# Stage borders of a two-layer streaming encoder: where the last block's norm sums go, how early the scaling runs, and how many residual slots there are

## What is computed

```python
for i in range(DEPTH):
    h = rms_norm(x, norm_g[i, 0])
    o = mixer(h)                                   # GLA for i = 0, SWA for i = 1
    x = x + rms_norm(o, norm_g[i, 1])
    h = rms_norm(x, norm_g[i, 2])
    x = x + rms_norm(squared_relu_mlp(h, w_up, w_down), norm_g[i, 3])
```

## Time and profile before

| | us |
|---|---|
| median of 3 runs | 2623.77 (2623.68 to 2635.75) |
| the profiled execution, whole | 2626.12 |
| its span | 2624.3 |
| TensorE busy in the span | 2509.7 (96%) |
| VectorE, ScalarE, GpSimd busy | 910.4, 842.0, 554.4 |
| mean granted TensorE clock | 0.98 |

### The profile page before, as it was taken

The page is one execution under the profiler, slowest core; times in us unless marked ns, Lnnn a source line. Parts: engine busy times, 40 slices in busy tenths (PEclk is TensorE's granted clock), DMA queues, the critical chain, the costliest instruction groups (busy, mean ns, idle before and its releaser), DMA issues.

```text
span 2624.3 us, 41637 instructions
## 1 busy us (share of the span) xinstructions
PE 2509.7 (96%) x17454; PEld 2370.0 (90%) x17454; DVE 910.4 (35%) x1785; ACT 842.0 (32%) x1666; POOL 554.4 (21%) x314
## 2 busy tenths in 40 slices
PE   6999999998999999999998999899899999999997
PEld 5878877798999999999998877689899999999996
DVE  6455454426322222222226344415422222212225
ACT  4445444526221221121125455536411211211121
POOL 1101010115221211221214211114312211212213
PEclk9999999999999999999998999899999999999998
DMA  3101010114111111111114200013211111111113
GB/s 107 41 10 47 26 40 17 43 45 147 62 46 42 47 40 48 40 48 40 60 33 135 67 26 26 29 33 116 82 47 43 41 47 41 47 40 48 40 61 125
DMA packets 63088, 139.05 MB, mean 53 GB/s; under 512 B 8688, under 2 KB 39920, under 8 KB 62960
## 3 DMA queue, kind: packets, MB, share of 16 engines
q1 hardware_dynamic: 33984, 103.60, 12.1%
q10 hardware_dynamic: 28976, 33.64, 4.2%
HBM read 117.81 MB, written 19.40 MB: 52 GB/s over the span
## 4 chain that ended last, share of the span: by engine, by line
PE 78%; ACT 3%; DVE 3%; issue 2%; ACTq 1%; DMA 0%; POOL 0%; DVEq 0%; POOLq 0%
PE banks L217 52%; PE banks L197 18%; PE banks L1860 1%; PE banks L1380 1%; PE banks L1361 1%; ACTq L339 1%; ACT norm_sq L464 1%; PE banks L1348 1%; PE banks L1388 0%; DVE norm_acc_x L542 0%; PE banks L2011 0%; PE banks L369 0%; PE banks L2014 0%; PE banks L1995 0%; ACT w_hi L153 0%
## 5 line engine op out<-in xcount | busy, mean ns | idle before, releaser
L160 POOL TENSOR_TENSOR w_lo<-w_raw,w_hi 128x1024 fp32r<-128x1024 f32 x168 | 414.9, 2473 | 1870.1 <-ACT w_hi L153 1870.1
L197 PE MATMUL banks<-h_hi,w_hi 128*128 128x384 f32 (+1 forms) x1224 | 432.8, 354 | 6.3 <-ACT gla_v_tok L2110 3.0
L197 PE MATMUL banks<-h_lo,w_hi 128*128 128x384 f32 (+1 forms) x1224 | 409.9, 335 | 0.0
L197 PE MATMUL banks<-h_hi,w_lo 128*128 128x384 f32 (+1 forms) x1224 | 409.1, 334 | 0.0
L153 ACT CAST w_hi<-w_raw 128x1024 fp32r<-128x1024 f32 x180 | 186.9, 1046 | 461.6 <-DMA w_raw<-in_units 461.6
L217 PE MATMUL banks<-h_hi,w_hi 128*128 128x384 f32 (+1 forms) x1368 | 301.8, 329 | 0.0
L217 PE MATMUL banks<-h_hi,w_lo 128*128 128x384 f32 (+1 forms) x1368 | 301.4, 328 | 0.0
L217 PE MATMUL banks<-h_lo,w_hi 128*128 128x384 f32 (+1 forms) x1368 | 301.4, 328 | 0.0
L217 PE MATMUL banks<-mlp_a_hi,w_hi 128*128 128x384 f32 (+1 forms) x1344 | 296.5, 329 | 1.5 <-issue 1.3
L217 PE MATMUL banks<-mlp_a_lo,w_hi 128*128 128x384 f32 (+1 forms) x1344 | 295.1, 327 | 0.0
L217 PE MATMUL banks<-mlp_a_hi,w_lo 128*128 128x384 f32 (+1 forms) x1344 | 295.0, 327 | 0.0
(11 more groups left out here) (199 smaller groups left out, 3183.4 us busy)
## 6 DMA issues: line engine op xcount, KB each, us to landing
w_raw<-in_units SPq DMA_DIRECT2D x180, 512.0 KB, 3.5
x_scratch<-y ACTq DMA_DIRECT2D x48, 192.0 KB, 1.9
norm_x<-x_scratch ACTq DMA_DIRECT2D x48, 192.0 KB, 2.7
x_scratch<-y ACTq DMA_DIRECT2D x24, 160.0 KB, 1.8
norm_x<-x_scratch ACTq DMA_DIRECT2D x24, 160.0 KB, 2.6
y<-in_x SPq DMA_DIRECT2D x16, 192.0 KB, 4.9
norm_x<-in_x ACTq DMA_DIRECT2D x16, 192.0 KB, 2.7
out_y<-y SPq DMA_DIRECT2D x16, 192.0 KB, 3.2
```

Source lines behind the costliest of these rows:

```text
L160: c.nc.gpsimd.tensor_tensor(c.w_lo[:, s], c.w_raw[:, s], c.w_hi[:, s].bitcast(F32), ALU.subtract).then_inc(self.ready, 1)
L197: mm = chip.nc.tensor.matmul(out, w, x, start=(first and n == 0), stop=(last and n == 2))
```

## The change

1. In borders 1 to 4, block 2's sums and its spread move from bank 5 to the squares' bank 4 (`norm_bank`), and the wait of `bank_left` goes.
2. On TensorE, in the middle borders: block 1's spread one place later; the second norm's sums of block 0 at the end of the last wave and not behind the first job of the next stage; behind that job the spread of it and block 2's sums; block 2's spread behind job (0, 1) and not (0, 3); block 1's second sums behind (0, 3) and not (1, 0).
3. On DVE and ACT the scaling and splitting of block 1 starts earlier in the last wave, `root_x(0)` and `inverse_x(0)` stand ahead of the last two weight units or one of them, `root(2)` and `inverse(2)` stand in job (0, 0), and block 2's steps begin in job (0, 1). For b > 0 the DVE sums the squares of x and makes the low part one step later behind the scaling (`lag`).
4. In borders 1 and 3 the odd tiles of block 0 are also split by DVE and not POOL (`low_by_vector`).
5. In border 4 there are nine slots for x: five more in the MLP's buffer `act`, loaded by `load_more_x` before the last wave. Block 1's steps begin after job (2, 3) and not (2, 4), and `root(2)` stands ahead of the remaining `high` calls.

```diff
-    X_SLOTS = 4
+    X_SLOTS, X_MORE = 4, 5
+    def norm_bank(self, b):
+        return SQ_BANK if b == 2 and not self.first else RS_BANK + b % 2
     def low_by_vector(self, b, k):
-        return self.first or (b > 0 and k % 2 == 1)
+        return self.first or (k % 2 == 1 and (b > 0 or not self.after_mlp))
     def sums(self, pe, b):
-        if b == 2:
-            self.bank_left(pe)
+        if b == 2 and self.first:
+            pe.wait_ge(self.s.scaled, KT)
...
-        if (b, q) == (2, 3):
+        if (b, q) == ((2, 3) if self.last else (2, 4)):
             self.spread(pe, 1)
+        if self.middle and (b, q) == (2, 7):
+            self.sums_x(pe, 0)
     def tensor_in_first_wave(self, pe, b, j):
         if (b, j) == (0, 0):
-            self.sums_x(pe, 0)
-        if (b, j) == (0, 1):
             self.spread_x(pe, 0)
-        if (b, j) == (0, 2):
             self.sums(pe, 2)
-        if (b, j) == (0, 3):
+        if (b, j) == (0, 1):
             self.spread(pe, 2)
...
     def scalar_before_first_wave(self, act, next_unit):
         ws.high(act, next_unit + 2)
-        self.high(act, 1, 0)
+        self.root_x(act, 0)
+        if self.after_mlp:
+            self.high(act, 1, 2)
         ws.high(act, next_unit + 3)
-        self.high(act, 1, 1)
-        self.root_x(act, 0)
-        self.high(act, 1, 2)
         self.high(act, 1, 3)
+        self.high(act, 1, 4)
         self.keep_block(act, 0)
...
     def scalar_after_all(self, act):
-        for k in range(6, KT):
+        self.root(act, 2)
+        for k in range(4, KT - 1):
             self.high(act, 1, k)
-        self.root(act, 2)
-        for k in range(KT - self.X_SLOTS):
-            self.high(act, 2, k)
```

More of the change, by code:

```diff
@@ L294, in gained @@
     def gained(self, b, k):
-        n = self.added * (NB * KT - KT) + self.count_alike(b, k)
+        n = sum(self.LOWS_BY_GPSIMD[:self.norm]) + self.count_alike(b, k)
         return n, self.s.sq[:, n % 2, 0:WIDTH[b]]
@@ L304, in h_ready @@
         if self.low_by_vector(b, k):
-            engine.wait_ge(self.s.lo_done_v, n if self.first else NB * KT + self.added * KT + n)
+            engine.wait_ge(self.s.lo_done_v, sum(self.LOWS_BY_VECTOR[:self.norm]) + n)
         else:
-            engine.wait_ge(self.s.lo_done, self.added * (NB * KT - KT) + n)
+            engine.wait_ge(self.s.lo_done, sum(self.LOWS_BY_GPSIMD[:self.norm]) + n)
     def bank_free(self, pe, j):
@@ L674, in vector_in_last_wave @@
                 self.steps(dve, 0, 5, KT)
[L675 to L676 removed]
+            if b == 2 and 3 <= q < 7:
+                self.steps(dve, 1, 2 * q - 6, 2 * q - 4)
         elif b == 2:
[L678 removed]
+            if q < 4:
+                self.step(dve, 0, q + 5)
             if q == 4:
+                self.steps(dve, 0, 9, 11)
+            first = 5 if self.after_mlp else 4
+            if q >= first:
+                self.step(dve, 1, q - first)
+            if q == 7 and not self.after_mlp:
+                self.step(dve, 1, 4)
+            if q == 5:
                 self.chip.stream.first_low(dve, self.next_unit)
[L681 removed]
+            if q == 7:
                 self.chip.stream.first_low(dve, self.next_unit + 1)
@@ L1021, in scalar @@
         ws.high(act, u0 + 8 * last + 7)
+        if self.after.last:
+            act.wait_ge(self.a_ready, 4 * last + 2)
+            self.after.load_more_x(act)
         for b in range(NB):
```

118 lines of the change are left out of this document (68 added, 50 removed).

## The result

The changed kernel takes 2610.44 us (median of 5 runs) against 2625.25 us for the kernel before in the same sitting. The ratio is 0.9943, with a 95% interval of 0.9926 to 0.9960: 14.8 us less, where 31 were forecast. The time lies 2.4 us above the range. The span of the profiled execution falls from 2624.3 to 2608.4 us, by 15.9.

A forecast was written before the change was run, and what follows sets the result against it. TensorE, working in 96% of the span, was taken as the bound. Middle borders' 25.3 us (38.9 less new waits and a clock fall) plus border 4's 6.0 made 31.3 us less: forecast 2592 us, range 2579 to 2608.

The forecast's parts named there:

- What can go, 38.9 us: Middle borders: TensorE's waits and time lost at half clock, removable 12.4, 15.0 and 11.5 us, together 38.9.
- block 1's spread no longer waits: Middle borders: twelve more products ahead of this spread, 1.7 us, remove its waits of 1.47 and 1.61 us.
- The new wait at block 0's second spread, 2.2 us: Middle borders: root_x(0) on ScalarE comes late, so TensorE waits 2.2 us in each, without a clock fall.
- The walk: Middle borders: ScalarE's durations summed from block 1's root at 608.65, 14.0 us to root_x, then 7.4 to block 2's spread.
- The new wait at block 2's spread, 0.6, 3.1 and 0.6 us: Middle borders: 7.4 us from root_x to spread against TensorE's 6.8; in border 2, 9.9 against 6.8.
- The prediction's own sign of being wrong: Any border: TensorE waiting over 4 us would show the prediction wrong.
- The clock: Middle borders: half clock only behind border 2's 3.1 us wait, none behind the 2.2 us waits.
- The 2.75: Border 2: 2.75 us added for a half-clocked stretch behind the wait at block 2's spread.
- The low parts moved to VectorE: Borders 1 and 3: eight instructions of 0.61 us, four in each, costing TensorE nothing; cover lost 4.9 us.
- Border 4: Program's end: sums 0.4 us earlier, root 2.5, spread 0.5 and waits for x 2.6, sum 6.0 us saved.
- The wait moves: Rival, 18%: middle borders keep about 3 us at both new waits plus clock falls, 29 us against 38.9; 2608 us.
- the 61%: Chance given to the forecast itself, a time of 2584 to 2600 us.

The follow-up runs named there:

- e1: Changed kernel with block 2's inverse ahead of the first taken job on VectorE and ScalarE in the middle borders; 2606.06 us.
- e4: Changed kernel with one ScalarE instruction moved: block 2's root ahead of the first job's square and cast; 2604.71 us.
- e5: Changed kernel with block 1's four odd low parts per middle border made by GpSimd, not VectorE, and four more casts on ScalarE; 2604.11 us.
- e9: e7 with block 2's root ahead of job 0's activation and block 1's second variance and root ahead of block 2's steps; 2592.72 us.
- e8: Changed kernel with block 0's second norm earlier, block 2's inverse right behind it, and block 1's second variance and root ahead of block 2's steps; 2601.55 us.
- e7: Changed kernel with block 2's spread one job later on TensorE, behind job (0, 2), in the middle borders; 2599.48 us.

## Why the prediction was wrong, point by point

- **What can go, 38.9 us, and that block 1's spread no longer waits**: right. The waits there are 0, 0.20 and 0.
- **The new wait at block 0's second spread, 2.2 us**: 0.66, 2.02 and 1.27, without a fall of the clock, as taken. The walk's terms give 13.3 us from block 1's root to root_x (14.0 less 0.7; the 622.3 written down has 13.65), and the trace has 607.29 to 620.60, 13.3. ScalarE was held up for only 0.7 us there, so a sum of its durations was a fair walk, though so close a fit is in part luck: two of the five highs were shorter by a cast, and one more job was taken out. In border 1 the wait is 1.5 us shorter than forecast because the walk started from block 1's root at 608.65, the place in the kernel before, and this root now comes at 607.29.
- **The new wait at block 2's spread, 0.6, 3.1 and 0.6 us: this step failed.** It was 4.38, 7.97 and 4.37. The walk from root_x to the spread gave 7.4 us in border 1, where the trace has 11.4. It summed ScalarE's durations again and let VectorE come in only with 0.55 for the job, where VectorE was the path: busy without a gap for 9.2 us from root_x's end to the end of the variance, against the 5.1 of the walk's cast, two highs, copy and job. ScalarE was held up for 3.5 us ahead of `keep_block(0)`: 0.91 for a weight's landing, 0.65 and 1.14 for VectorE's sums, 0.43 for a GpSimd add, 0.37 of issue. VectorE took the job 0.9 us behind the copy, because of a low part of 1.29 us. In border 2 the same walk gave 9.9 and the trace 14.9: 2.44 and 0.70 of waiting for sums, a low part of 1.16 and the queries' bias of 0.95 ahead of the job, and 1.29 of cache loads. There VectorE was busy from 1408.1 to 1419.7 with one gap of 0.34 us. That the place of the inverse on the queues is what made the spread late is shown by e1, where no such wait is left. VectorE's queue should have been walked beside ScalarE's, each start being the later of the two. The prediction's own sign of being wrong, a wait over 4 us at a border, stands in all three.
- **The clock**: a fall behind the wait in border 2 was forecast, and none elsewhere. That followed from the waits: there was one behind each of the three, 2.7, 1.5 and 1.5 us of TensorE's time. The 2.75 for the one in border 2 was too much: half of the fall lay inside the wait (the clock was down from 1418.9, the spread started at 1422.73).
- **The sum.** With these waits and falls the same books give 38.9 - 27.1 + 5.8 = 17.6 us, near the 15.9 of the spans. The middle borders became 11.1 us shorter, so that 0.7 us of these 11.8 is all that is not accounted for there.
- **The low parts moved to VectorE** cost TensorE nothing that shows where they were moved to (block 0's, ahead of 614): the one at 605.18 took 0.62 us, and the GpSimd add that started beside it took 1.34 and not 1.0. But the low parts of block 1, which stood on VectorE before, took part in the late diagonal at 1.19 and 1.29 us, twice the median. The trace agrees with the rule of the Trainium skill that the prediction quotes (SBUF — State Buffer, "SBUF: two separate sides"): of the 32 instructions of that line the shortest took 0.545 us, the median 0.613 and the longest 1.295; the one of 1.19 us ran beside a GpSimd add (623.57 to 624.58), the one of 1.29 (from 628.16) beside the second of two adds (628.05 to 629.03). In these the engine that starts second is the one that takes longer: the add at 605.33 started behind the low part, the low part at 623.81 behind the add. GpSimd in border 1:

```profile
605.33 1.34 POOL L629 TENSOR_TENSOR y<-y,norm_x 128x384 f32<-128x384 f32 x1
...
623.57 1.01 POOL L629 TENSOR_TENSOR y<-y,norm_x 128x384 f32<-128x384 f32 x1 [2.22 <-DVE y L614]
...
627.08 1.95 POOL L629 TENSOR_TENSOR y<-y,norm_x 128x384 f32<-128x384 f32 x2
```

- **Border 4**: 6.0 forecast, 5.8 found, and part by part: the sums 0.39 earlier (0.4), the root 2.49 (2.5), the spread 0.54 shorter (0.5), the waits for x gone (2.6). The last add ends 2.5 us ahead of the end, and the stores take nothing back.
- **The rivals.** "The wait moves" came nearest: it gave 29 us of new waits and falls against the 27.1 found, and 2608 us. That the totals are so near is luck in part: it had about 3 us at either spread and two falls in border 2, and the trace has 0.7 to 2.0 us at the first, 4.4 to 8.0 at the second and one fall each. Its chance of 18% was too low, as the 61% rested on a walk of one engine.

## What to carry to other kernels

Where two engines hand single buffers to and fro (here a square into one bank, its sum out of it), walk both queues together: an engine with time to spare on its own can still be late by half of its stretch (ScalarE was held up for 3.5 us of 7.4), and the other's queue can be the path. Put the short steps on which TensorE waits (variance, root, diagonal) at the place where their input is ready, not behind the taking of a job that they don't need. When a mended wait turns up at the next step with the time unchanged, look for the next queue place before calling it a floor: five orders ended at 2599.5 to 2601.6 us, and the two that mended the next place took 2589 and 2593.

## What the runs showed of the hardware

- **The length of a wait doesn't tell whether the clock falls.** Behind waits of 1.32 us (e4, border 3), 1.91 (e5, border 1) and 1.81 (e9, border 2) the granted clock was 0.50 for 3 to 7 us. Behind 2.02 us (changed kernel, border 2) and 2.31 (e8, border 1) it stayed at 1.00. One trace has both: in e7 a wait of 1.87 us at the same spread was followed by half clock in border 1 and by full clock in border 3 (TensorE's timeline, and stretches of 1 us as above). In the middle borders of all these traces each wait of 2.35 us or more was followed by half clock, and the shorter ones went either way in kernels that differ in a few instructions. What else decides is not settled by these runs.

```profile
644.89 1.58 PE L399 MATMUL banks<-norm_diag_x,all_ones 128*128 128x384 f32 x2 [1.87 <-DVE norm_diag_x L602]
...
1830.77 0.91 PE L399 MATMUL banks<-norm_diag_x,all_ones 128*128 128x384 f32 x2 [1.87 <-DVE norm_diag_x L602]
```

```profile
645.00:646.00 1.00, 1.00 (x3) 0.50 0.63 193
...
1831.00:1832.00 1.00, 1.00 (x5) 1.00 0.54 173
```

- **The cost of a fall depends on what comes next.** In e5 half clock lay where TensorE would have waited for a diagonal, and border 1 became shorter (77.6 us) than the changed kernel's (79.9), whose fall came behind its longest wait, where TensorE had work.
- **Neighbours in time cost VectorE up to double**: the low part of h took 0.61 us as a rule, and 1.19 and 1.29 behind a GpSimd add that had started first; the low part of a weight took 1.21 us, and 1.99 in e5 at 624.91, beside a GpSimd add from 624.82 on.
